# Two-layer hybrid decoder step: normalised x held two tiles ahead, channel-major projections, and score masks added on VectorE with the maximum

## The chip, the cores and the metric

The kernel runs on one core of one Trainium2 chip (trn2) as one program on all five engines: TensorE (PE), VectorE (DVE), ScalarE (ACT), GpSimd (POOL) and SyncE (SP, which only issues DMAs here). The metric is the device time of one execution in microseconds, the median of several executions. All arithmetic is float32, apart from a bfloat16 copy of the score masks and of the identity.

## What is computed

Two layers run over a prompt of 2,048 rows of 1,024 channels and over 8 single-row samples. The prompt is nearly all of the work. Per layer, cut to what matters:

```
def hybrid_layer(x, c, pos0, k_buf, v_buf, shift_prev, wkv0, conv_buf, h0, lp):
    mod = jax.nn.silu(c) @ lp["w_mod"] + lp["b_mod"]
    shift_m, scale_m, gate_m = jnp.split(mod, 3, axis=-1)
    h = rmsnorm(x, lp["norm_pre"]) * (1.0 + scale_m[:, None]) + shift_m[:, None]
    proj = h @ lp["w_in"]                                  # 1024 -> 2880
    qa, ka, va, ga, pb, gb, xc, gc = jnp.split(proj, IN_OFFSETS, axis=-1)
    ya = swa_banded(rope(qa), rope(ka), va, sinks) * jax.nn.silu(ga)     # group A
    yb = rwkv7_time_mix(pb, gb, shift_prev, wkv0, lp)                    # group B
    yc = rglru_mix(xc, gc, conv_buf, h0, pos0, lp)                       # group C
    y = jnp.concatenate([ya, yb, yc], axis=-1) @ lp["w_out"]             # 1024 -> 1024
    return x + gate_m[:, None] * rmsnorm(y, lp["norm_post"])

def sink_attention(s, mask, sinks, v, eq):       # A: 128 queries against 256 keys, 8 heads
    s = jnp.where(mask, s, -jnp.inf)
    m = jnp.maximum(jnp.max(s, axis=-1, keepdims=True), sink)
    p = jnp.exp(s - m)
    denom = jnp.sum(p, axis=-1, keepdims=True) + jnp.exp(sink - m)
    return jnp.einsum(eq, (p / denom).astype(v.dtype), v)

def wkv_step(s, inp):                            # B: one token, state 64 x 64 for each of 4 heads
    sa = jnp.einsum("bhvk,bhk->bhv", s, -kk)
    s = s * w[:, :, None, :] + sa[..., None] * (kk * a)[:, :, None, :] + v[..., None] * k[:, :, None, :]
    return s, jnp.einsum("bhvk,bhk->bhv", s, r)
# C: u = causal conv of width 4; gates = sigmoid(u @ block-diagonal w); h_t = a_t h_(t-1) + b_t
```

## The kernel before

The prompt is cut into 16 tiles of 128 rows per layer, 32 tiles in all. Both weight matrices of a layer lie in SBUF. Before the first tile of a layer the modulation vectors are computed; after its last tile the 8 samples are worked through. One loop iteration is one tile n, in which some steps of tile n+1 are already done (those under `if ahead`). Each engine has its own list of instructions, written out by hand in `program`; the lists meet at semaphores (`s[...]`), and an engine carries out its list strictly in the written order. So the order of the source is the order of the work.

A float32 product is two MATMUL records in the profile. A stationary operand (a weight load) is at most 128 x 128, and the moving operand at most 512 columns wide. `half` is the two halves of the partitions; products of 64 x 64 are issued for both halves in turn.

On PE one tile of before runs as follows:

- `vbT`, the low-rank products (L512) and the sum of squares of k (L517);
- projections by `fill` (L419: the tile's transposed input `hT` is stationary, the weights move, rows of tokens come out): Q (512 wide), XC with VA (384), GB with GC (512, with the product for the bonus, L528, in between); the two XC blocks are then transposed back to channels (L415);
- the small matrices of group B (L545 to L555) and five rounds that invert a triangular matrix: `squares(level)` (L566) and `multiply(level)` (L579), between which lie fill steps of GA, the gate products of group C (L602), the transposes of GB and GC and of q and k (L415). After each round ACT and DVE copy the squares out of PSUM (`power`, `power_T`) and DVE adds the product to Q (`product`, L1315);
- scores: `scores(j)` for j = 0, 1. For each of two banks a bfloat16 product of the identity with the mask (L627, 512 columns) sets the bank to 0 or -1e30, and two products of q and k (L630, 256 columns) accumulate on it. DVE takes the maximum (`maxima`, L1367) and ACT the exponentials straight from PSUM (`exps`, L1035);
- the recurrence over two chunks of 64 rows: `right_side` (L662, L664), DVE copies it with the sign changed (`rhs`, L1380), `solve` (L673), ACT copies, `next_state` and `outputs` (L685 to L703), DVE scales the state (`state`); between them the transposed probabilities (`probs`, L415) and `values` (L652);
- for tile n+1: x is normalised by DVE (`x_norm`, L1207) from the root that ACT took, transposed (`x_lo`, `x_hi`), and projected: R and K (512 wide), then V, WA and KA (448 wide), and 7 of those blocks transposed to channels after ACT has copied them out (`channels_rk`, `channels_vw`);
- the output projection `project` (L757), two halves of 512 columns, then the post-norm: ACT squares, DVE forms the mean, ACT the root, DVE the reciprocal (L1452 to L1456) and the output rows (L1457 to L1460), the last of which signals `o_ready`.

## Time and profile before

| what | value |
|---|---|
| runs | 3259.58, 3265.19, 3268.19 us |
| median | 3265.19 us |
| profiled execution | 3271.33 us |
| its span, first to last instruction | 3269.5 us |
| PE busy | 3017.4 us (92%) |
| DVE busy | 1750.7 us (54%) |
| ACT busy | 1429.8 us (44%) |
| POOL busy | 0.2 us, 4 instructions |

Busy time is the union of an engine's instructions. PE's matmuls are pipelined: a record lasts longer than the distance to the next one, so what a product costs is read from the start of a group to the start of the next, not from its duration. A wait that an engine spends while the end of its last record is still modelled as busy shows less than its full length for the same reason.

### The profile page before, as it was taken

The numbers are of one execution on the slowest core, as the hardware profiler recorded it, in microseconds if no ns is written. First come the engines' busy times: TensorE is split into PE (matmuls) and PEld (weight loads), VectorE is DVE, ScalarE is ACT, GpSimd is POOL, SyncE is SP. The second block draws the span as 40 slices with busy tenths as digits, with TensorE's granted clock in tenths as the row PEclk, the third lists the DMA queues.
The fourth block names the chain that finished last, engine by engine and source line by source line (L and its number), as shares of the span: only waits on it lengthen the run. The fifth ranks groups of instructions, "written<-read, shape, count | busy, mean of one in ns | idle before, by whom it ended". The sixth has DMA issues, their size and how long they took to land.

```text
span 3269.5 us, 62255 instructions
## 1 busy us (share of the span) xinstructions
PE 3017.4 (92%) x24404; PEld 1852.7 (57%) x24404; DVE 1750.7 (54%) x4385; ACT 1429.8 (44%) x3055; POOL 0.2 (0%) x4
## 2 busy tenths in 40 slices
PE   4899999999999999998649999999999999999986
PEld 3555556666655555665335555566666655555654
DVE  1455555556555555555414555555566555555554
ACT  0444445445544444544204444454455544445432
POOL 0000000000000000000000000000000000000000
PEclk7999999999999999999769999999999999999996
DMA  9000000000000000000370000000000000000001
GB/s 371 8 20 20 20 20 19 7 20 20 20 13 20 20 20 20 19 7 14 119 289 2 20 20 20 20 19 7 20 20 20 13 20 20 20 20 19 12 9 39
DMA packets 36847, 116.07 MB, mean 36 GB/s; under 512 B 13104, under 2 KB 16304, under 8 KB 36016
## 3 DMA queue, kind: packets, MB, share of 16 engines
q1 hardware_dynamic: 29136, 89.20, 7.8%
q10 hardware_dynamic: 7648, 26.04, 2.1%
q8 instruction: 38, 0.62, 0.1%
q14 instruction: 25, 0.20, 0.0%
HBM read 96.83 MB, written 18.41 MB: 35 GB/s over the span
## 4 chain that ended last, share of the span: by engine, by line
PE 75%; DVE 15%; issue 6%; DMA 2%; ACT 1%; ACTq 0%; DVEq 0%; SPq 0%
PE G L419 37%; PE M L757 14%; PE M L415 5%; PE G L652 4%; DVE small L1367 2%; DMA RB<-in_w_mod 2%; PE M L579 2%; PE M L566 2%; PE G L425 2%; DVE W L1291 1%; DVE RA L1332 1%; DVE Q L1315 1%; PE M L602 1%; PE M L512 1%; PE M L545 1%
## 5 line engine op out<-in xcount | busy, mean ns | idle before, releaser
L419 PE MATMUL G<-w_in,hT 128*128 128x512 f32 (+2 forms) x3072 | 1296.6, 572 | 3.1 <-DVE hT L1212 3.1
L419 PEld LDWEIGHTS G<-w_in,hT 128*128 128x128 f32 x3072 | 571.4, 191 | 552.8 <-issue 474.9
L757 PE MATMUL M<-w_out,yT 128*128 128x512 f32 x1024 | 454.1, 597 | 5.2 <-DVE yT L1446 5.2
L757 PEld LDWEIGHTS M<-w_out,yT 128*128 128x128 f32 x1024 | 191.3, 192 | 223.9 <-issue 223.9
L1224 DVE TENSOR_TENSOR xs<-pB 128x768 f32<-128x768 f32 x32 | 30.7, 959 | 395.8 <-ACT pB L938 395.8
L1315 DVE TENSOR_TENSOR Q<-Q,M 64x256 f32<-64x256 f32 x320 | 133.8, 418 | 119.4 <-PE M L579 115.3
L566 PE MATMUL M<-W 64*64 64x64 f32 x4608 | 163.5, 218 | 7.8 <-DVE W L1291 7.8
L566 PEld LDWEIGHTS M<-W 64*64 64x64 f32 x4608 | 149.4, 135 | 11.3 <-issue 11.3
L630 PE MATMUL M<-kT,stA 64*128 64x256 f32 x512 | 144.3, 402 | 0.0
L652 PE MATMUL G<-Vt,RB 128*128 128x64 f32 x1024 | 127.9, 278 | 0.0
L579 PEld LDWEIGHTS M<-Q,W 64*64 64x64 f32 x2560 | 88.2, 134 | 68.2 <-issue 68.2
L652 PEld LDWEIGHTS G<-Vt,RB 128*128 128x128 f32 x1024 | 119.1, 191 | 4.3
L1035 ACT ACTIVATE RA<-M,small 128x256 f32<-128x256 f32 x256 | 117.3, 472 | 0.0
L984 ACT ACTIVATE W<-M 64x512 f32<-64x512 f32 (+1 forms) x160 | 87.6, 547 | 66.6 <-PE M L566 66.6
L1070 ACT ACTIVATE RB<-M 128x512 f32<-128x512 f32 x32 | 19.1, 598 | 210.3 <-PE M L757 210.3
L972 ACT ACTIVATE xcb<-M 128x256 f32<-128x256 f32 x32 | 12.4, 386 | 222.8 <-PE M L415 222.8
L579 PE MATMUL M<-Q,W 64*64 64x64 f32 x2560 | 107.5, 223 | 2.5
L630 PEld LDWEIGHTS M<-kT,stA 64*128 64x128 f32 x512 | 85.6, 186 | 36.4 <-issue 29.0
L1309 DVE COPY W<-M 64x512 f32<-64x512 f32 (+1 forms) x160 | 102.0, 638 | 6.3
L1291 DVE TENSOR_TENSOR W<-M,nstrict 64x512 f32<-64x512 f32 x64 | 44.1, 689 | 111.1 <-PE M L545 110.6
L415 PE MATMUL M<-cst,RA 128*128 128x128 f32 x642 | 87.8, 284 | 6.4 <-DVE stA L1579 6.4
L927 ACT ACTIVATE stB<-G 128x320 f32<-128x320 f32 x32 | 14.0, 438 | 171.8 <-PE G L419 171.8
(403 smaller groups left out, 4559.2 us busy)
## 6 DMA issues: line engine op xcount, KB each, us to landing
w_in<-in_w_in SPq DMA_DIRECT2D x2, 11520.0 KB, 33.3
xa<-in_x_prompt SPq DMA_DIRECT2D x16, 512.0 KB, 3.6
RA<-in_w_mod ACTq DMA_DIRECT2D x16, 512.0 KB, 6.3
W<-in_w_mod ACTq DMA_DIRECT2D x16, 512.0 KB, 6.5
w_out<-in_w_out SPq DMA_DIRECT2D x2, 4096.0 KB, 36.7
G<-in_x_prompt SPq DMA_DIRECT2D x16, 512.0 KB, 3.3
x_mid<-RA SPq DMA_DIRECT2D x16, 512.0 KB, 2.8
xa<-x_mid SPq DMA_DIRECT2D x16, 512.0 KB, 3.7
```

The lines of the kernel that those rows point to most:

```text
L415: return nc.tensor.transpose(out, in_, ident[0:rows, 0:rows])
L419: last = mm(out[:, 0:width], hT[:, k, :], Win[:, k, col:col + width], start=k == 0, stop=k == KC - 1)
L566: last = mm(m[r, 256 * w + CH * u:256 * w + CH * u + CH], NW[r, 1 - w, u, :], NW[r, w, u, :], start=True, stop=True)
L579: last = mm(m[r, 256 + CH * u:256 + CH * u + CH], NW[r, 1, u, :], Q[r, u, :], start=True, stop=True)
L630: last = mm(m[:, 256 * c:256 * c + 256], qT[HD * g:HD * g + HD, 2 * j + c, :], kT[HD * g:HD * g + HD, :], start=False, stop=True, skip_gro ...
L652: last = mm(G1[:, HD * (4 * j + k):HD * (4 * j + k) + HD], PT[:, f, k, :], Vt[:, f, HD * g:HD * g + HD], start=f == 0, stop=f == 1)
L757: last = mm(o[:, :], yT[:, k, :], Wout[:, k, 512 * h:512 * h + 512], start=k == 0, stop=k == KC - 1)
L984: A(NW[half[0], w:], M0[half[0], 256 * w:512].rearrange("p (w u c) -> p w u c", u=U, c=CH), ACT.Copy).then_inc(s["inv_act"], 1)
L1035: last = A(Pm[:, j, k, :], m[:, 256 * (k // 2):256 * (k // 2) + 256], ACT.Exp, bias=small[:, 16 + 4 * j + k:17 + 4 * j + k], scale=SCALE, ...
L1291: last = tt(NW[r], m[r, :].rearrange("p (w u c) -> p w u c", w=2, c=CH), over(nstrict[r], 2, U), ALU.mult)
L1309: cp(NW[half[1], w:], M1[half[1], 256 * w:512].rearrange("p (w u c) -> p w u c", u=U, c=CH))\
L1315: last = tt(Q[r, :, :], Q[r, :, :], m[r, 256:512].rearrange("p (u c) -> p u c", c=CH), ALU.add)
```

## The change

Seven things are changed, in one go.

1. **x two tiles ahead.** `xn` is gone: DVE normalises x in place in `xa` (`x_mean`), for tile n+2, late in tile n. `hT` has two buffers, and the loop body is two tiles long. `x_lo` and `x_hi` of tile n+1 move from the recurrence to before `multiply(4)` and before `scores(0)`.
2. **Channel-major projections.** A new `channels` takes the weights as stationary operand and the 128 columns of `hT` as moving operand, so channels come out directly. R, K, V, XC, GB and GC (12 blocks of 128) are made so; Q and GA stay as `fill` of 512 columns, VA becomes a `fill` of 128, and WA with KA one of 192. Of the 13 transposes back to channels (4 for R and K, 3 for V and WA, 2 for XC, 4 for GB and GC) one is left (`wab`, for WA).
3. **Order on PE.** GB and GC are no longer projected early; their four blocks (`gates(0..3)`) stand inside the recurrence. The gate products of group C come after six of the eight steps of Q. The steps `vbT`, low rank and sum of squares of tile n+1 (`front`) stand between the halves of `project`.
4. **Masks on DVE.** The four mask products are gone. `maxima` is four `tensor_tensor_reduce`, each of which adds the mask to 256 columns, writes them to `Pm` in SBUF and gives their maximum. ACT takes the exponentials from `Pm`. In `scores` the two halves of the partitions alternate.
5. **Roots on POOL.** The roots of the pre-norm, of group B's norm and of the post-norm are a power of -0.5 on POOL, with their small sums before it. DVE's reciprocals after them are gone. Group B's squares move from ACT to DVE.
6. **Operands of B ahead.** The decays (ACT, 3 table loads) and `operands` (DVE) of tile n+1 stand at the end of tile n, ahead of the output rows.
7. **Smaller moves.** `rope` moves from before the inversion to after `power_T(2)`; the gates' silu on GA is split into a copy and a later silu; `power_T` now waits for the product of the round before.

The core of the diff, other moves left out:

```
+            def channels(out, H, col, width):
+                for k in range(KC):
+                    last = mm(out[0:width, :], Win[:, k, col:col + width], H[:, k, :], start=k == 0, stop=k == KC - 1)
+                return last
...
-                    fill(G0, C_Q, 512, range(KC)).then_inc(s["q_mm"], 1)
-
-                    fill(G1, C_XC, 384, range(KC)).then_inc(s["xv_mm"], 1)
-
-                    pe.wait_ge(s["q_out"], DONE(n))
-                    fill(G0, C_GB, 512, range(0, 5))
...
+                    for j in range(2):
+                        channels(G1[:, P * j:P * j + P], H, C_XC + P * j, P)
+                    fill(G1[:, 2 * P:3 * P], H, C_VA, P, range(KC)).then_inc(s["xv_mm"], 1)
+
+                    pe.wait_ge(s["rk_out"], DONE(n))
+                    fill(G0, H, C_Q, 512, range(0, 6))
+                    pe.wait_ge(s["conv_ready"], DONE(n))
+                    for k in range(4):
+                        last = mm(M3[:, P * k:P * k + P], gatew[:, k, :], lu[:, k % 2, :], start=True, stop=True)
...
-                        for g, m in ((0, ma), (1, mb)):
-                            mm(m[:, :].rearrange("p (c k) -> p c k", c=2), identb[:, :], over(mk[:, :], 1, 2),
-                               start=True, stop=False, skip_group_check=True)
-                            for c in range(2):
-                                last = mm(m[:, 256 * c:256 * c + 256], qT[HD * g:HD * g + HD, 2 * j + c, :],
-                                          kT[HD * g:HD * g + HD, :], start=False, stop=True, skip_group_check=True)
...
+                        for c in range(2):
+                            for g, m in ((0, ma), (1, mb)):
+                                last = mm(m[:, 256 * c:256 * c + 256], qT[HD * g:HD * g + HD, 2 * j + c, :],
+                                          kT[HD * g:HD * g + HD, :], start=True, stop=True)
...
-                        for g, m in ((0, ma), (1, mb)):
-                            last = red(mx[:, :, g], m[:, :].rearrange("p (c k) -> p c k", c=2), AX_X, ALU.max)
+                        dve.sem_inc(L["dve_w"], 1)
+                        for c in range(2):
+                            for g, m in ((0, ma), (1, mb)):
+                                last = nc.vector.tensor_tensor_reduce(
+                                    out=Pm[:, j, 2 * c + g, :], in0=m[:, 256 * c:256 * c + 256], in1=mk[:, :], scale=1.0,
+                                    scalar=NEG, op0=ALU.add, op1=ALU.max, accum_out=mx[:, c, g:g + 1])
...
+                    pool.wait_ge(s["o_squared"], DONE(n))
+                    link(tt(small[:, 5:6], small[:, 3:4], small[:, 4:5], ALU.add))
+                    pool.sem_inc(L["pool_w"], 1)
+                    link(ts(small[:, 5:6], small[:, 5:6], D * EPS, None, ALU.add))
+                    tt(small[:, 60:61], small[:, 5:6], minus, ALU.pow).then_inc(s["o_root"], 1)
...
-                    dve.wait_ge(s["o_squared"], DONE(n))
-                    link(tt(small[:, 5:6], small[:, 3:4], small[:, 4:5], ALU.add))
-                    link(ts(small[:, 5:6], small[:, 5:6], 1.0 / D, EPS, ALU.mult, ALU.add))
-                    assert link.k == OVAR, link.k
+                        operands(n + 1)
+
                     dve.wait_ge(s["o_root"], DONE(n))
```

**The recurrence on PE.** Before, from the second pair of scores to the first transposed probabilities (`mk,identb` is the mask product, `RH,Q` the solve, `cst,RA` the transposes of the probabilities):

```order
L627 MATMUL M<-mk,identb 128x512 [waits l_zeros]
L630 MATMUL M<-kT,stA 128x256 x2
L627 MATMUL M<-mk,identb 128x512
L630 MATMUL M<-kT,stA 128x256 x2
L662 MATMUL M<-S,kr 64x64 [waits s_qbd]
...
L664 MATMUL M<-Vst,G 64x64 x2
L668 REGISTER_ALU
L673 MATMUL M<-RH,Q 64x64 [waits s_rh_ready]
L673 MATMUL M<-RH,Q 64x64 x3
L415 MATMUL M<-cst,RA 128x128 [waits s_exp0]
```

and in the changed kernel (`hT,w_in` is `gates(0)`):

```order
L634 MATMUL M<-kT,stA 128x256 [waits s_inv_dve,s_inv_act,l_zeros]
L634 MATMUL M<-kT,stA 128x256 x3
L665 MATMUL M<-S,kr 64x64 [waits s_q_dve]
...
L667 MATMUL M<-Vst,G 64x64 x2
L438 MATMUL G<-hT,w_in 128x128 [waits s_hT_hi]
L438 MATMUL G<-hT,w_in 128x128 x7
L671 ISA
L676 MATMUL M<-RH,Q 64x64 [waits s_rh_ready]
L676 MATMUL M<-RH,Q 64x64 x3
L429 MATMUL M<-cst,RA 128x128 [waits s_exp0]
```

The masks have left, and eight products of 128 columns now stand between the right side and the solve that waits for DVE's copy of it.

**The gate products of group C on PE.** Before, in the second round of the inversion (`RA,gatew` are the gate products, `cst,stA` the transposes of GB and GC):

```order
L566 MATMUL M<-W 64x64 x16
L602 MATMUL M<-RA,gatew 128x128 [waits s_bt_out,s_conv_ready]
L602 MATMUL M<-RA,gatew 128x128 x3
L415 MATMUL M<-cst,stA 128x128 [waits s_gbc_out]
L415 MATMUL M<-cst,stA 128x128 x3
L419 MATMUL G<-w_in,hT 128x512 x2
```

and in the changed kernel, at the start of the tile:

```order
L438 MATMUL G<-hT,w_in 128x128 [waits s_pB_ready]
L438 MATMUL G<-hT,w_in 128x128 x15
L433 MATMUL G<-w_in,hT 128x128 x8
L433 MATMUL G<-w_in,hT 128x512 [waits s_rk_out]
L433 MATMUL G<-w_in,hT 128x512 x5
L544 MATMUL M<-RA,gatew 128x128 [waits s_conv_ready]
L544 MATMUL M<-RA,gatew 128x128 x3
```

The gate products, and the wait for the convolution with them, have moved ahead of the inversion, behind XC, VA and six steps of Q.

**The two maxima on DVE** of the changed kernel. Each `tensor_tensor_reduce` is compiled to two instructions, shown as ISA; the product of the fifth round (L1345) now stands ahead of them, and the transposed halves of hT (L1242) ahead of that:

```order
L1242 TENSOR_SCALAR hT<-G,gs,mod 128x128 [waits s_xT_hi]
L1242 TENSOR_SCALAR hT<-G,gs,mod 128x128 x3
L1345 TENSOR_TENSOR Q<-Q,M 64x256 [waits s_q_mm5]
L1345 TENSOR_TENSOR Q<-Q,M 64x256
L1394 ISA RA,small<-M,mk 128x256 [waits s_s0_mm]
L1394 ISA small 128x1
```

Before, the maxima of the first pair stood ahead of that product:

```order
L1367 TENSOR_REDUCE small<-M 128x2 [waits s_s0_mm]
L1367 TENSOR_REDUCE small<-M 128x2
...
L1371 TENSOR_SCALAR small<-small 128x4 [waits l_dve_t]
L1372 TENSOR_TENSOR small<-prm,small 128x4
L1315 TENSOR_TENSOR Q<-Q,M 64x256 [waits s_q_mm5]
L1315 TENSOR_TENSOR Q<-Q,M 64x256
```

## Rows read from the trace of the kernel before

**Rows 1.** The page's part 1, and TensorE's granted clock over 40 slices.
```profile
PE 3017.4 (92%) x24404; PEld 1852.7 (57%) x24404; DVE 1750.7 (54%) x4385; ACT 1429.8 (44%) x3055; POOL 0.2 (0%) x4
...
PEclk7999999999999999999769999999999999999996
```

**Rows 2.** Sums by stretch: both tile loops (from:to, length, busy times, clock, DMA).
```profile
150.00:1580.00 1430.00, 1378.82 (x11171) 844.29 (x11174) 806.06 (x1995) 666.87 (x1436) 0.00 (x0) 0.99 0.06 19
...
1760.00:3190.00 1430.00, 1379.85 (x11351) 847.32 (x11349) 813.60 (x2010) 678.51 (x1457) 0.00 (x0) 0.99 0.05 17
```

**Rows 3.** Waits of PE, all tiles: total us, times, longest.
```profile
PE M L602 <- DVE xcb L1335: 31.0, 32, 1.0
PE M L673 <- DVE RH L1380: 24.8, 32, 0.8
```

**Rows 4.** PE in order of time, gate products of two successive tiles (start, length, records).
```profile
774.38 1.16 PE L602 MATMUL M<-RA,gatew 128*128 128x128 f32 x8 [0.97 <-DVE xcb L1335]
775.38 0.60 PE L415 MATMUL M<-cst,stA 128*128 128x128 f32 x4
...
864.85 1.16 PE L602 MATMUL M<-RA,gatew 128*128 128x128 f32 x8 [0.97 <-DVE xcb L1335]
```

**Rows 5.** PE in order of time, scores to first probabilities, then `x_lo`.
```profile
789.69 0.39 PE L627 MATMUL M<-mk,identb 128*128 128x512 bf16 x1
790.01 1.13 PE L630 MATMUL M<-kT,stA 64*128 64x256 f32 x4
791.07 0.39 PE L627 MATMUL M<-mk,identb 128*128 128x512 bf16 x1
...
792.71 0.33 PE L662 MATMUL M<-S,kr 64*64 64x64 f32 x4 [0.20 <-DVE Q L1315]
...
793.08 0.31 PE L664 MATMUL M<-Vst,G 64*64 64x64 f32 x4
794.17 0.45 PE L673 MATMUL M<-RH,Q 64*64 64x64 f32 x8 [0.78 <-DVE RH L1380]
794.55 1.09 PE L415 MATMUL M<-cst,RA 128*128 128x128 f32 x8
...
796.90 0.28 PE L703 MATMUL M<-Vst,G 64*64 64x64 f32 x4
797.32 0.66 PE L415 MATMUL G<-cst,RA 128*128 128x128 f32 x4
```

**Rows 6.** PE in order of time, `values`, projection of R and K, transposes.
```profile
803.89 2.00 PE L652 MATMUL G<-Vt,RB 128*128 128x64 f32 x16
805.73 7.08 PE L419 MATMUL G<-w_in,hT 128*128 128x512 f32 x16
812.65 0.60 PE L415 MATMUL M<-cst,stA 128*128 128x128 f32 x4
813.09 0.60 PE L415 MATMUL M<-cst,W 128*64 128x128 f32 x4
```

**Rows 7.** DVE in order of time: post-norm, output rows; product, maxima of a pair.
```profile
744.62 0.16 DVE L1452 TENSOR_TENSOR small<-small 128x1 f32<-128x1 f32 x1 [2.44 <-ACT RB L1075]
...
746.40 0.75 DVE L1457 SCALAR_TENSOR_TENSOR RA<-M,small,gp 128x512 f32<-128x512 f32 x1
...
748.99 1.19 DVE L1245 COPY Vst<-M 64x128 f32<-64x128 f32 x4
...
791.72 0.84 DVE L1315 TENSOR_TENSOR Q<-Q,M 64x256 f32<-64x256 f32 x2
...
794.05 1.29 DVE L1367 TENSOR_REDUCE small<-M 128x2 f32<-128x512 f32 x2
```

**Rows 8.** ACT in order of time: one exponential and its accumulator read; a table load.
```profile
744.61 1.28 ACT L1077 ACT_TABLE_LOAD   x1
...
791.95 0.46 ACT L1035 ACTIVATE RA<-M,small 128x256 f32<-128x256 f32 x1
792.31 0.19 ACT L1035 ACTIVATION_READ_ACCUMULATOR RA<-M,small 128x1 f32 x1
```

647 lines of the change are left out of this document (338 added, 309 removed).

## Prediction

> **What bounds the kernel now.** I read the page's busy shares first [rows 1]: PE is busy for 92% of the span, DVE for 54%, ACT for 44%. The two tile loops alone, taken from the sums by stretch [rows 2], have PE at 1378.8 of 1430 us, 96%, at a granted clock of 0.99 (the 2.4 GHz level). Between two successive tiles the same instruction starts at 774.38 and at 864.85 [rows 4], so a tile takes 90.5 us, and 32 of them are 2,895 of the 3,269.5 us. PE is busy in about 87.2 us of a tile and idle in 3.3. So PE's list sets the time, and there are two ways to gain: less work on it, or fewer waits in it. A faster DVE or ACT gains nothing by itself. The clock cannot rise further.
>
> Then the waits of PE in a tile. The list of waits has two that occur 32 times [rows 3]: the gate products of group C wait for the convolution on DVE (31.0 us in all, 0.97 each), and the solve waits for DVE's sign change (24.8 us, 0.78). Both show a little short, since the modelled end of the record before covers part: from the start of L664 at 793.08, which takes about 0.12, to the solve at 794.17 there is 1.0 us [rows 5]. Two smaller ones are in the order of time: 0.2 before the right side, and about 0.3 before `x_lo` (from 796.90 to 797.32 less one group of 0.12) [rows 5]. With some tenths before the first squares and before the second right side, about 3.3 us.
>
> **PE's work, part by part.** Prices are distances from start to start, for one tile.
>
> Transposes: 13 go, 1 comes. Four take 813.09 - 812.65 = 0.44 us [rows 6], so 12 x 0.11 = **-1.3**.
>
> Masks: a mask product starts at 789.69, the score product after it at 790.01 [rows 5]. Four of 0.32: **-1.3**. The two kinds of products also alternate between two shapes of the array, and the first score record after a mask comes late, so up to -1.7.
>
> Narrow blocks: the 8 steps of 512 columns for R and K take 812.65 - 805.73 = 6.92 us [rows 6], or 1.73 for 128 columns. A block of 128 in `channels`, or VA's as `fill`, is 8 products of two records, each with a weight load of 128 x 128 of its own and 128 moving columns. No row has just that. The nearest from below is a transpose, 0.11 a record; from above the gate products, 8 records in 775.38 - 774.38 = 1.00, 0.125 each, with a late start in it [rows 4]. `values` has the same weight load, two records a product, and half the columns: 16 records in 1.84 us, 0.115 [rows 6]. It is nearest, because the load, and not the columns, seems to set its pace; I take 0.115. A block is then 1.84, and 13 of them (12 and VA) cost 13 x 0.11 = **+1.4**, between +0.4 (0.11) and +3.5 (0.125). WA and KA at 192 columns are taken at their share of the old 448.
>
> Shape changes: `gates(0)` stands between products of 64 x 64. Two changes of shape more, about 0.1 to 0.15 each: **+0.3**.
>
> Work together: -1.3 - 1.3 - 0.4 + 1.4 + 0.3, about **-1.3** (with the masks at -1.7).
>
> **PE's waits.** The wait for the convolution goes: in the new list XC, VA and six steps of Q stand before the gate products. From the end of `project`, PE has 3 x 1.84 + 6 x 0.865 = 10.7 us of its own. DVE needs the post-norm's root, the output rows (746.40 to 748.99, 2.6) [rows 7], the copies of V (1.2) [rows 7] and the convolution (about 2.8). With ACT's square of 0.8 before, 7.4 us are fixed, and a root chain of up to about 2.7 us on POOL is hidden after semaphores. **-1.0**.
>
> The wait of the solve goes: `gates(0)`, 1.84 us, stands in it. **-1.0**. The one before `x_lo` goes, since x is ready a tile earlier (**-0.3**), those before the two right sides too (**-0.4**): the fifth product now comes before the maxima on DVE, and `gates(1)` covers the state.
>
> One wait comes. The exponentials of the first pair are late, because `product(5)` now stands ahead of the maxima. From the end of `multiply(5)`: the product 0.85 [rows 7], four mask-and-maximum instructions, three small ones 0.35, the exponentials 4 x 0.45 + 0.2 = 2.0 [rows 8], hops 0.3. An add-and-maximum of 256 columns from PSUM is in no row. Two rows bound it: half a reduction of 512 columns (0.65 / 2 = 0.32) and the sum of half-width add (0.42, half of L1315's pair) and a whole reduction of its own (0.65), 1.07 [rows 7]. ACT's accumulator read, 0.19 and half hidden [rows 8], is what its second instruction is like, so I take 0.42 + 0.13 = 0.55. The chain is 0.85 + 2.2 + 0.35 + 2.0 + 0.3 = 5.7 us. PE has in that time scores (about 1.9 without masks), right side 0.5, `gates(0)` 1.84, solve 0.4, together 4.6. **+1.0 to +1.1**.
>
> Waits together: -1.0 - 1.0 - 0.3 - 0.4 + 1.05, about **-1.7**; following all four lists through one tile by these prices, with the late starts, gives PE **86.7 us** a tile where the same walk through the old lists gives 90.2 (trace: 90.5). That is -3.5, against -3.0 by the two sums above; the walk has the smaller waits that I rounded away. I take -3.5.
>
> What must stay hidden in it: `rope` (2.7 us on DVE) in the second round lies beside fill steps of GA and the third squares; table loads of ACT (1.28 each [rows 8]) fall from 12 to 8 a tile, the one in the third round ends before the third squares; decays, three loads and `operands` of tile n+1 lie beside the second half of `project`, 6.9 us, and end about 2 us after it, beside XC. On SP, x of tile n+2 is asked for after `x_hi` and is there long before ACT's square. If one of ACT's copies in the inversion were late by a load, PE would lose up to 1.3 a tile.
>
> A rule on the scores. Row first: the four records of a bank's scores come one after another, 790.01 to 791.07, 0.21 to 0.25 each plus a change of shape [rows 5]; all of them lie in one half of the rows of the array. In the change the halves alternate. The Trainium skill (TensorEngine Tiling (Array Packing), Key Properties) says that tiles of different row groups work independently, in parallel. By the rule a pair of scores would take about 1.1 us and not 1.9, and PE's busy time would fall by 1.7 a tile; but the same products and maxima on DVE then end the wait, so a tile would be 86.6 and not 86.7, and the time 3 us less.
>
> **The sum.** 32 x -3.5 = -112. The first tile of each layer now has decays and operands before its loop, some of it bare: +3 a layer, +6. Span 3269.5 - 112 + 6 = 3163.5. The profiled execution took 1.8 us more than its span and was 6.1 us above the median of the runs: 3163.5 + 1.8 - 6.1 = 3159. I round to **3158 us**, 3.3% less.
>
> **Rivals.**
>
> *The root chain on POOL is long.* Three POOL instructions with a power in the last. POOL has done only 4 fills of 0.05 us [rows 1], so no row bounds it above. From below it is about 0.5: the same sums on DVE take 0.16 each [rows 7]. Before, 1.8 us passed from the sum (744.62) to the output rows (746.40) [rows 7]. DVE waits for the root in order; behind it are output rows, the copies of V and the convolution, and PE's gate products wait for these. Up to 2.7 us nothing shows. At 4.5 us a tile costs 1.8 more: 3158 + 58 = 3216. The other roots have over 10 us of cover.
> The Trainium skill (GPSIMD Engine Reference, on how an instruction executes) gives POOL two software dispatch hops where VectorE has one, which speaks for this rival; it has no price for a power, and no run shows one yet.
>
> *Slower: the same mechanism further on.* Above 2.7 + 3.5 = 6.2 us for the three instructions the tile is longer than before. At 7.5 us each tile is 4.8 above forecast: 3158 + 154 = 3312. For it speaks that a power is no simple operation; against it that there is one value a partition.
>
> *The maxima are slow.* At 1.07 us for each of the eight instead of 0.55, the chains through them to the solve and to the exponentials grow by 2.1 and PE has nothing to put there: 3158 + 32 x 2.1 = 3225. It is at its worst 1.5 a piece, where the gain is gone.
>
> *The narrow blocks are not as cheap, or the waits merely move.* At 0.125 a record the blocks cost 2.1 more: 3225. A table load of ACT bare in the inversion in each tile: 3199. Both: 3266, no gain.
>
> **Chances.** Forecast 0.66 (own range 3105 to 3195); POOL long but hidden in part 0.11; POOL over 6.2 us 0.06; maxima slow 0.09; narrow blocks or a load bare 0.08. The low end has every unknown at its lower bound: narrow blocks at 0.11 (-1.0), maxima at 0.42 (-0.5), halves in parallel: 85.2 a tile, 3110; I set 3105. The high end takes in the rivals that are still faster: 3230. Outside lie 0.06 above for POOL, 0.04 for two rivals together and some below. A difference of 0.3% (10 us) is what a measurement can tell: faster 0.88, within 0.04, slower 0.08.
>
> **What would show it.** In the profile of the changed kernel: tiles 86 to 87 us apart; PE's wait before the gate products and before the solve gone; a wait of about 1 us before the first probabilities, ended by ACT's exponentials; 128-column records 0.11 to 0.125 apart; ACT with 8 loads a tile; the three POOL instructions within 2.7 us between ACT's second square and the output rows. Wrong if the gate products still wait for the convolution (POOL), if the solve waits for the sign change behind long maxima, or if a copy of ACT ends waits in the inversion.

## The result, and the profile after

The changed kernel takes 3142.7 us, the median of four runs (3135.95 to 3146.62). The kernel before took 3266.5 beside it (3259.58 to 3268.19). The ratio is 0.962, 95% interval 0.960 to 0.9645: 3.8% less, 15 us below the forecast of 3158 and inside its range. The profiled execution has a span of 3134.2 us, where that of before had 3269.5.

The page's part 1, then the sums over one tile (from:to, length, busy times, granted clock, DMA), of the changed kernel:

```profile
PE 2903.3 (93%) x29012; PEld 2200.6 (70%) x29012; DVE 1736.6 (55%) x4549; ACT 1216.0 (39%) x2739; POOL 108.2 (3%) x229
```
```profile
700.64:787.25 86.61, 84.43 (x862) 64.74 (x860) 51.48 (x133) 36.56 (x84) 3.38 (x7) 1.00 0.06 20
```

The same sum for the tile of before in [rows 4]:

```profile
774.38:864.85 90.47, 88.07 (x716) 53.91 (x717) 51.94 (x129) 43.36 (x93) 0.00 (x0) 1.00 0.05 18
```

Compare the last two. The tile is 3.86 us shorter (90.47 - 86.61). PE is busy 3.64 us less in it, and idle for 2.18 us instead of 2.40. So nearly all of the gain is work taken off PE's list, and hardly any of it is waiting. That is not how the forecast had it.

PE's waits, all tiles (total us, times, longest), of the changed kernel. The two of before [rows 3] were 31.0 for the convolution and 24.8 for the solve:

```profile
PE M L429 <- ACT RA L1022: 33.0, 32, 1.0
PE M L592 <- issue: 16.8, 32, 1.1
PE M L665 <- DVE Q L1345: 13.6, 30, 0.5
...
PE M L544 <- DVE xcb L1311: 6.7, 14, 0.6
```

Two waits of 32 times went; two of 32 and one of 30 came ("issue" at L592 is the semaphore of `power_T(5)`, below). The gate products still wait for the convolution, in 14 of 32 tiles.

PE in order of time from the first scores to the first probabilities, in the changed kernel; it answers to [rows 5]:

```profile
740.75 1.14 PE L634 MATMUL M<-kT,stA 64*128 64x256 f32 x8
742.37 0.68 PE L592 MATMUL M<-Q,W 64*64 64x64 f32 x16 [0.49 <-issue]
742.98 1.14 PE L634 MATMUL M<-kT,stA 64*128 64x256 f32 x8
744.57 0.33 PE L665 MATMUL M<-S,kr 64*64 64x64 f32 x4 [0.45 <-DVE Q L1345]
...
745.18 2.05 PE L438 MATMUL G<-hT,w_in 128*128 128x128 f32 x16
747.16 0.45 PE L676 MATMUL M<-RH,Q 64*64 64x64 f32 x8
748.65 1.09 PE L429 MATMUL M<-cst,RA 128*128 128x128 f32 x8 [1.03 <-ACT RA L1022]
```

The eight records of a pair of scores take about 1.1 us. In before a bank with its mask takes 791.07 - 789.69 = 1.38 [rows 5], a pair 2.76. The solve at 747.16 follows the block gates(0) without a wait.

DVE and ACT beside it:

```profile
739.88 0.85 DVE L1345 TENSOR_TENSOR Q<-Q,M 64x256 f32<-64x256 f32 x2 [0.99 <-PE M L592]
740.76 0.86 DVE L1382 TENSOR_TENSOR_SCAN lh<-RA,hcar 128x128 f32<-128x128 f32 x2
...
741.84 0.43 DVE L1339 COPY W<-M 64x256 f32<-64x256 f32 x1
742.30 1.37 DVE L1242 TENSOR_SCALAR hT<-G,gs,mod 128x128 f32<-128x128 f32 x4
743.59 0.84 DVE L1345 TENSOR_TENSOR Q<-Q,M 64x256 f32<-64x256 f32 x2
744.46 0.42 DVE L1394 CUSTOM_DVE_ANT_0 RA<-M,mk 128x256 f32<-128x256 f32 x1
...
744.81 0.42 DVE L1394 CUSTOM_DVE_ANT_0 RA<-M,mk 128x256 f32<-128x256 f32 x1
```
```profile
746.42 0.21 ACT L1020 ACTIVATE small<-small 128x4 f32<-128x4 f32 x1 [4.47 <-DVE small L1401]
```

DVE does not stop from 739.88 to the end of the maxima. All three new waits of PE hang on this list: the fifth multiply (L592) waits for L1339 (`power_T(5)`), the right side (L665) for L1345 (`product(5)`), and the probabilities (L429) for ACT, which begins when the maxima are through.

The distance from one tile to the next is 86.61 us and 87.3 to 87.4 us in turn, through both loops; below, a tile of the second kind is called slow. There are 12 of them among the 28 distances of the two layers. DVE at the start of a slow tile, the copies of V and the end of the convolution:

```profile
801.31 1.19 DVE L1298 COPY Vst<-M 64x128 f32<-64x128 f32 x4 [1.99 <-issue]
...
805.12 0.17 DVE L1311 COPY xcb<-xcb 128x6 f32<-128x6 f32 x1
```

At its loop's jump back DVE stands still for 1.99 us, waiting for no engine. The convolution then ends at 805.3 and PE's gate products start at 805.35, with a wait of 0.56. The kernel before has one tile in its loop's body, so it jumps back after every tile, and there DVE goes from the last output row straight to the copies of V, which start at 748.99 [rows 7]:

```profile
747.85 1.23 DVE L1460 TENSOR_TENSOR RA<-RA,G 128x1024 f32<-128x1024 f32 x1
```

So the stop came with the body of two tiles. What it consists of is not shown.

### The profile page after: what moved, and what is told of

Its sections match the earlier page's. It is cut to its first block, busy times and chain, and to the rows that moved or that the text cites. A ratio compares the mean times of both kernels' runs of the same rounds, so it can differ in the third digit from the quotient of the medians.

```text
span 3134.2 us, 71309 instructions
## 1 busy us (share of the span) xinstructions
PE 2903.3 (93%) x29012; PEld 2200.6 (70%) x29012; DVE 1736.6 (55%) x4549; ACT 1216.0 (39%) x2739; POOL 108.2 (3%) x229
## 4 chain that ended last, share of the span: by engine, by line
PE 66%; issue 18%; DVE 9%; DMA 3%; ACT 3%; POOL 1%; ACTq 0%; DVEq 0%; POOLq 0%; SPq 0%
PE G L438 15%; PE G L433 13%; PE M L765 8%; PE M L579 4%; PE G L655 4%; PE M L429 3%; PE M L592 2%; ACT RA L1022 2%; PE G L444 2%; PE M L433 2%; DVE Q L1345 1%; DVE hT L1242 1%; PE M L605 1%; PE M L560 1%; DVE RA L1394 1%
## 5 line engine op out<-in xcount | busy, mean ns | idle before, releaser
L438 PE MATMUL G<-hT,w_in 128*128 128x128 f32 x6144 | 739.0, 279 | 4.6 <-DMA w_in<-in_w_in 2.9
L438 PEld LDWEIGHTS G<-hT,w_in 128*128 128x128 f32 x6144 | 714.4, 193 | 26.5 <-issue 19.7
L433 PE MATMUL G<-w_in,hT 128*128 128x512 f32 (+1 forms) x1536 | 538.4, 494 | 0.0
L433 PEld LDWEIGHTS G<-w_in,hT 128*128 128x128 f32 x1536 | 236.6, 191 | 159.5 <-issue 152.9
L1345 DVE TENSOR_TENSOR Q<-Q,M 64x256 f32<-64x256 f32 x320 | 133.6, 417 | 117.6 <-PE M L592 114.5
L592 PEld LDWEIGHTS M<-Q,W 64*64 64x64 f32 x2560 | 88.2, 134 | 82.6 <-issue 82.6
L1022 ACT ACTIVATE RA<-RA,small 128x256 f32<-128x256 f32 x256 | 125.9, 495 | 0.0
L592 PE MATMUL M<-Q,W 64*64 64x64 f32 x2560 | 107.5, 223 | 16.8 <-issue 16.8
L1468 DVE COPY Ep<-M 64x256 f32<-64x256 f32 x64 | 26.7, 417 | 150.2 <-PE M L429 149.7
L429 PE MATMUL M<-cst,RA 128*128 128x128 f32 (+1 forms) x514 | 70.7, 280 | 39.4 <-ACT RA L1022 33.0
L1339 DVE COPY W<-M 64x512 f32<-64x512 f32 (+1 forms) x160 | 102.2, 639 | 5.7
L1271 DVE TENSOR_TENSOR_SCAN W<-cst,W 128x256 f32<-128x256 f32 x32 | 22.1, 692 | 147.8 <-ACT W L952 147.8
L926 ACT ACTIVATE pB<-G 128x512 f32<-128x512 f32 x32 | 19.1, 597 | 210.4 <-PE G L438 210.4
L1394 DVE CUSTOM_DVE_ANT_0 RA<-M,mk 128x256 f32<-128x256 f32 x256 | 93.3, 421 | 2.0
```

Of the source, the lines that this page charges most:

```text
L429: return nc.tensor.transpose(out, in_, ident[0:rows, 0:rows])
L433: last = mm(out[:, 0:width], H[:, k, :], Win[:, k, col:col + width], start=k == 0, stop=k == KC - 1)
L438: last = mm(out[0:width, :], Win[:, k, col:col + width], H[:, k, :], start=k == 0, stop=k == KC - 1)
L592: last = mm(m[r, 256 + CH * u:256 + CH * u + CH], NW[r, 1, u, :], Q[r, u, :], start=True, stop=True)
L1022: last = A(Pm[:, j, k, :], Pm[:, j, k, :], ACT.Exp, bias=small[:, 16 + 4 * j + k:17 + 4 * j + k], scale=SCALE, accum_out=small[:, 24 + 4 * ...
L1339: cp(NW[half[1], w:], M1[half[1], 256 * w:512].rearrange("p (w u c) -> p w u c", u=U, c=CH))\
```

## The experiments

Times are medians of four runs (ten for gates0_after_outputs, one for masks_between). The kernel before, run beside them, took 3264.1 us with halves_apart, masks_back and the two gates0 kernels, 3264.4 with wide_blocks, conv_first, pool_longer and scans_late, and 3259.9 with the others. "Tile" is the distance between the starts of `project` in two successive tiles (fast, slow of a pair) in the profile.

| kernel | median us | tile us |
|---|---|---|
| changed | 3142.7 | 86.61, 87.3 |
| halves_apart | 3147.4 | 86.61, 87.3 |
| masks_back | 3135.9 | 86.28, 87.0 |
| masks_between | 3173.8 (one run) | 87.70, 88.4 |
| gates0_after_solve | 3216.6 | 88.8, 89.4 |
| gates0_after_outputs | 3256.8 | 89.9, 91.3 |
| wide_blocks | 3132.4 | 86.12, 86.8 |
| conv_first | 3131.4 | 86.61, 86.61 |
| pool_longer | 3186.1 | 87.05, 90.7 |
| scans_late | 3108.5 | 85.57, 86.3 |
| masks_scans | 3115.3 | 85.68, 86.4 |
| combo_b | 3088.6 | 85.27, 85.27 |
| combo_c | 3081.2 | 84.97, 84.97 |

The tile is the sharper measure: the ratios of halves_apart, masks_back, wide_blocks and conv_first to the kernel before have 95% intervals that overlap the changed kernel's 0.960 to 0.9645, so the medians do not tell these from it. The start is what blurs the medians. The first `project` begins between 170 and 192 us in these profiles, and ahead of every tile PE waits 25 to 49 us for the DMA of `w_mod`, which the edits do not touch. In gates0_after_solve, gates0_after_outputs and pool_longer some tiles differ from the figures of the table (two of pool_longer take 89.0 where the others in their place take 90.7).

### Masks and scores

**halves_apart**

```diff
-                        for c in range(2):
-                            for g, m in ((0, ma), (1, mb)):
+                        for g, m in ((0, ma), (1, mb)):
+                            for c in range(2):
```

> The changed kernel with one thing undone: in a pair of scores the two products of one half of the rows stand together again, as before, instead of alternating. Theory A (the halves run in parallel, but DVE's chain product, maxima, exponentials sets when the first probabilities start): PE's busy time goes up by about 0.8 us a pair, 1.6 a tile, 50 us in all; the first pair's 0.8 goes mostly into the wait of 0.49 before the fifth multiply, the second's into the 0.45 before the right side and the 1.03 before the probabilities, so the time stays within 10 us of the changed kernel's 3143 us. Theory B (pairs take the same either way, the row groups do not overlap): PE busy unchanged too. Theory C (the pairs lie on the path): 0.8 to 1.6 us a tile, 3168 to 3194 us.

Tile 86.61, PE busy 2905.8 us against 2903.3. The pair's rows read the same, 1.14 us for eight records:

```profile
748.23 1.14 PE L634 MATMUL M<-kT,stA 64*128 64x256 f32 x8
```

Unchanged busy time was what theory B expected, but its reason, no overlap, does not hold. The trace has the eight records start in pairs, 13 ns apart, though the list has all of one half first. It does not name the half of a record, but before the change, where one half stood alone between two masks, its records started 0.22 to 0.32 us apart, so the two of a pair must be of different halves. They overlap in either order. The alternation that the change wrote does nothing.

**masks_back**

```diff
+                        for m in (ma, mb):
+                            mm(m[:, :].rearrange("p (c k) -> p c k", c=2), identb[:, :], over(mk[:, :], 1, 2), ...)
...
-                                last = nc.vector.tensor_tensor_reduce(...)
+                            last = red(mx[:, :, g], m[:, :].rearrange("p (c k) -> p c k", c=2), AX_X, ALU.max)
...
-                            last = A(Pm[:, j, k, :], Pm[:, j, k, :], ACT.Exp,
+                            last = A(Pm[:, j, k, :], m[:, 256 * (k // 2):256 * (k // 2) + 256], ACT.Exp,
```

> The changed kernel with part 4 undone but for the order of the halves: the mask is a bfloat16 product on TensorE again, DVE takes two maxima of 512 columns, ACT takes the exponentials from PSUM. Theory of the record's sum (a mask product is 0.32 us of PE's list, four a tile, with shape changes up to 1.7): 1.3 to 1.7 us a tile slower, 3185 to 3197 us. Rival (before the probabilities PE waits 0.49, 0.45 and 1.03 us for DVE and ACT anyway, and DVE's two reductions at 0.65 take what its four masked maxima at 0.345 do, 1.3 against 1.4): PE's busy time goes up by 1.3 or more a tile, about 45 us, and the time stays within 10 us of 3143.

PE's wait before the probabilities, all tiles of masks_back:

```profile
PE M L429 <- ACT RA L1026: 21.3, 32, 0.7
```

The theory of the sum fails and the rival holds on time: 3135.9 us, with the waits of 0.49 and 0.45 gone. PE's busy time rises by 28.6 us (2931.9), and not by the 45 of the rival. The tile is 0.33 us shorter, and so is the wait for the exponentials, 0.70 where the changed kernel has 1.03. The chain to them is shorter without the masks in it: from the first maximum to `rhs` DVE takes 1.67 us (757.73 to 759.40) where it took 1.85 (744.46 to 746.31), and ACT takes 1.91 for the exponentials, straight from PSUM, where it took 2.08 from SBUF.

**masks_between** is masks_back with the loops of before: mask, two products, mask, two products.

> The changed kernel with the scores exactly as before the change: the mask product of a bank directly ahead of its two score products, so that a mask product of all 128 rows of the array stands between the products of the two halves. With both mask products first, a pair's scores took 0.87 us for 8 records, two at a time; with the halves apart but no mask between them they took the same. Theory A (a product over all rows between the halves keeps them from overlapping): a pair takes 1.8 to 1.9 us again, PE's busy time is 25 to 30 us above that with both masks first (2932), the time within 10 us of it, since the fifth product on DVE is not ready earlier. Theory B (it makes no difference): busy 2932 within 5.

PE in order of time, masks_back and then masks_between, one pair of scores each:

```profile
756.25 0.61 PE L633 MATMUL M<-mk,identb 128*128 128x512 bf16 x2
756.79 1.13 PE L637 MATMUL M<-kT,stA 64*128 64x256 f32 x8
757.86 0.33 PE L668 MATMUL M<-S,kr 64*64 64x64 f32 x4
```
```profile
757.93 0.39 PE L633 MATMUL M<-mk,identb 128*128 128x512 bf16 x1
758.25 1.13 PE L636 MATMUL M<-kT,stA 64*128 64x256 f32 x4
759.31 0.39 PE L633 MATMUL M<-mk,identb 128*128 128x512 bf16 x1
759.63 1.13 PE L636 MATMUL M<-kT,stA 64*128 64x256 f32 x4
760.69 0.33 PE L667 MATMUL M<-S,kr 64*64 64x64 f32 x4
```

A pair is 1.61 us with both masks first and 2.76 with a mask between the halves. Without masks it is 1.1. So the two mask products cost 0.5 a pair, and the place of the second one another 1.15, since it keeps the halves from overlapping. That is 2.3 us a tile. Theory A on masks_between had the mechanism right and half of the size (PE busy 2999.7 us, 68 more than masks_back; its 0.87 for a pair's scores with the masks first is 1.07 in the rows above, 756.79 to 757.86). It was wrong on time, within 10 us: the tile is 87.70, 1.42 more than in masks_back, and the one run 38 us above that kernel's median. PE's list grew by 68 / 32 = 2.1 us a tile, and the only wait left to take that in was the 0.70 before the probabilities, which is gone in this run; here PE's own list is the path.

The masks as such are another matter. With both first on TensorE they are work for PE where it waited anyway. Moving them to DVE gained nothing by itself, it cost 0.33 us a tile (masks_back to the changed kernel); taking them from between the halves gained 1.42 (masks_between to masks_back).

### What the exponentials and the solve wait for

**gates0_after_solve**

```diff
-                    gates(0)
                     solve(0)
+                    gates(0)
```

> The changed kernel with the block gates(0) behind the first solve instead of before it. Theory of the record's sum (the wait of the solve, 1.0 us a tile, went away because gates(0) stands in it): the wait returns, 3143 + 32 = 3175 us. Rival (the exponentials' chain sets the start of the probabilities, and both places of gates(0) lie before it): PE waits about 1.1 us before the solve and nothing or 0.2 before the probabilities, the time stays within 10 us of 3143.

**gates0_after_outputs** puts gates(0) directly ahead of gates(1).

> The changed kernel with gates(0) behind the first outputs, next to gates(1), so that nothing of it stands before the first probabilities. Theory A (the probabilities start when the exponentials are done, whatever stands before): their start stays, PE idles there for the 1.8 us of the block besides, and the tile gets 1.8 us longer: 3143 + 58 = 3201 us. Theory B (PE's work alone counts, the block is only moved): 3143 within 10 us.

The time of both kernels lies above all theories on record (3216.6 us against 3175 and 3143, 3256.8 against 3201 and 3143). PE in gates0_after_solve, and the sums of short stretches around it (the number behind POOL's count is the granted clock):

```profile
514.12 0.69 PE L676 MATMUL M<-RH,Q 64*64 64x64 f32 x8 [1.78 <-DVE RH L1411]
514.75 3.19 PE L438 MATMUL G<-hT,w_in 128*128 128x128 f32 x16
517.77 1.04 PE L429 MATMUL M<-cst,RA 128*128 128x128 f32 x8
```
```profile
508.00:511.60 3.60, 2.71 (x32) 1.78 (x32) 3.48 (x11) 1.04 (x1) 0.00 (x0) 1.00 0.50 155
...
515.00:516.00 1.00, 1.00 (x6) 1.00 (x7) 0.87 (x7) 0.99 (x6) 0.00 (x0) 0.50 0.00 0
```

The wait is 1.78 and not 1.0, since on DVE the four maxima now stand between product(5), for which the right side waits, and `rhs`. After it TensorE's clock is at 0.50, the 1.2 GHz level, for about 3 us, and the block takes 3.02 from start to start where it took 1.98. That is so in most tiles: all 32 have the wait of 1.78, and in 29 the clock is down within the 3 us behind it. The rival was right that no wait is left before the probabilities: they are late by the slow block instead. Net of the 1.03 that is gone, the wait is 0.75 longer; the block adds 1.04 and the solve at the lower clock 0.25 (514.12 to 514.75, where it took 0.38 in [rows 5]), together 2.0 of the 2.2 us measured. In gates0_after_outputs a wait of 0.92 to 1.16 follows the 1.78, and the clock stays at 0.50 through the probabilities and the outputs: 3.3 us a tile in place of 1.8. Before the change, with waits of up to 1.0, the tile loops were at 0.99 [rows 2]. As a cover for the solve's wait gates(0) is worth 2.2 us a tile, twice what it was priced by; 0.75 of that is waiting and 1.3 is the clock.

**scans_late** moves the two scans and the copy of their last column on DVE:

```diff
                     product(4)
-                    for c in range(2):
-                        last = nc.vector.tensor_tensor_scan(lh[:, c, :], ...)
-                    link(last)
-                    cp(hcar[:, :].unsqueeze(2), lh[:, :, P - 1:P])
                     power_T(5)
...
                     rhs(0)
+                    for c in range(2):
+                        last = nc.vector.tensor_tensor_scan(lh[:, c, :], ...)
+                    link(last)
+                    cp(hcar[:, :].unsqueeze(2), lh[:, :, P - 1:P])
```

> The changed kernel with the two scans of group C and the copy of their last column (1.08 us on DVE) between the first rhs and the second maxima instead of ahead of power_T(5). Theory A (from the fourth product on, DVE's list is the path up to the first probabilities: power_T(5), h_hi, product(5), maxima, then ACT's exponentials): each of them starts 1.0 us earlier, PE's waits of 0.49 before the fifth multiply and of 0.45 before the right side go, and the tile is 1.0 us shorter, 3143 - 33 = 3110 us. Theory B (PE's own work sets the stretch, or the second maxima, now 1 us behind the first rhs, become late for the second exponentials): within 10 us of 3143.

```profile
741.70 0.68 PE L592 MATMUL M<-Q,W 64*64 64x64 f32 x16
...
743.42 0.33 PE L665 MATMUL M<-S,kr 64*64 64x64 f32 x4
...
747.50 1.09 PE L429 MATMUL M<-cst,RA 128*128 128x128 f32 x8 [1.03 <-ACT RA L1022]
```

Theory A, to 2 us: 3108.5, tile 85.57, both small waits gone, the one for the exponentials as it was. No instruction was removed. This shows that DVE's list is the path of this stretch, though DVE is busy for only 55% of the span.

**masks_scans** is masks_back and scans_late together.

> The changed kernel with the masks back on TensorE and the scans of group C behind the first rhs. With the masks back alone the tile was 0.33 us shorter than in the changed kernel, with the scans moved alone 1.04 shorter. Theory A (the mask products cost nothing there because PE waited before the fifth multiply; with the scans moved that wait is gone and the first pair's two mask products of 0.32 push the fifth multiply, product(5) and all behind it): 0.2 to 0.4 us a tile more than with the scans alone, about 85.9, 3118 us. Rival (the two effects add up): 85.2 a tile, 3098 us.

Tile 85.68. Adding the two effects would give 85.24, so they do not add, and the masks on TensorE now cost 0.11 instead of gaining 0.33. PE's list, now longer, starts the fifth multiply and the right side without a wait, and of the wait before the probabilities 0.22 is left (1.03 in scans_late). Theory A had the sign; the size is below its 0.2 to 0.4 by the tile, and at its low edge by the medians (6.8 us for 32 tiles).

### The narrow blocks, the convolution and POOL

**wide_blocks**

```diff
-                    for j in range(4):
-                        last = channels(G0[:, P * j:P * j + P], H, C_R + P * j, P)
-                    last.then_inc(s["rk_mm"], 1)
+                    fill(G0, H, C_R, 512, range(KC)).then_inc(s["rk_mm"], 1)
...
-                        return channels(G0[:, P * j:P * j + P], H, C_GB + P * j, P)
+                        return fill(G0, H, C_GB, 512, range(2 * j, 2 * j + 2))
```

> The changed kernel with R, K, GB and GC computed with the input as stationary operand and 512 moving columns (as before the change) but without the transposes, so that tokens and channels of these blocks are exchanged in what follows: it measures the pure price of the eight 128-column blocks. By the record's 0.115 us a record: 8 x 0.11 = 0.9 us of PE's list a tile, up to 28 us less, 3115. By 0.1125, as the changed kernel's rows read: 0.56 a tile, 14 to 18 us less, 3127. By the record's upper bound 0.125: 2.2 a tile, 3075 us. Half of the first gates block lies beside the exponentials' chain and gives nothing.

This kernel leaves out the transposes that the wide form needs, so what it computes is not the layer; only its time counts. Tile 86.12, 0.49 less, where 0.1125 us a record gives 0.56; the median is 10 us less, below the 14 to 18 of that line, and the prices of 0.115 and 0.125 are out. The changed kernel's own rows give the same: 64 records of R and K from 764.09 to 771.29, 7.20 us, where the wide form took 6.92 [rows 6]:

```profile
764.09 7.36 PE L438 MATMUL G<-hT,w_in 128*128 128x128 f32 x64
771.29 0.60 PE L429 MATMUL M<-cst,stA 128*128 128x128 f32 x4
```

**conv_first** moves DVE's four copies of V (L1298) behind the convolution, nothing else.

> The changed kernel with DVE's four copies of V (1.2 us) behind the convolution instead of ahead of it. In the changed kernel every second tile, the one whose start follows the loop's jump, is 87.3 to 87.4 us instead of 86.6: DVE stands still for 2.0 us at its jump, and the gate products wait 0.6 for the convolution. Theory A (that wait is all of the difference): the convolution ends 1.2 us earlier, all tiles are 86.6, 14 x 0.75 = 10 us less, 3133 us. Theory B (PE loses the 0.75 at a jump of its own, or in fetching instructions): the alternation stays and the time is unchanged.

Every tile is 86.61 us, and the median 11 us less. Theory A. DVE still stands still for 2.00 us at its jump, but the convolution now ends before PE needs it. So DVE's jump, by way of PE's wait for the convolution, is all of the alternation; PE jumps once in two tiles too and loses nothing.

**pool_longer**

```diff
+                    for _ in range(4):
+                        pool.sem_inc(L["pool_w"], 1)
+                        link(ts(small[:, 5:6], small[:, 5:6], 1.0, None, ALU.mult))
+                    pool.sem_inc(L["pool_w"], 1)
                     tt(small[:, 60:61], small[:, 5:6], minus, ALU.pow).then_inc(s["o_root"], 1)
```

> The changed kernel with four more multiplications by 1.0 in POOL's chain for the root of the post-norm, before the power: some 0.3 to 0.45 us each, so that the chain from ACT's second square to the root is 2.7 to 3.3 us instead of 1.6. The record's theory (up to 2.7 us the chain is hidden by PE's own work ahead of the gate products): 0 to 0.3 us a tile, 3143 to 3153 us. Rival (the cover is 1.4 us beyond what is used in one tile of two and nothing in the other, since DVE's jump of 2.0 us has used it up): 0 to 0.3 us in 16 tiles and 1.2 to 1.7 in 14, 3143 + 17 to 28 = 3160 to 3171 us.

POOL's chain in the changed kernel, then its first and last row in pool_longer, and there PE in a slow tile with the sums of the stretches behind the wait:

```profile
708.47 0.46 POOL L1144 TENSOR_TENSOR small<-small 128x1 f32<-128x1 f32 x1 [28.41 <-ACT RB L1063]
709.12 0.22 POOL L1146 TENSOR_SCALAR small<-small 128x1 f32<-128x1 f32 x1 [0.20 <-POOL small L1144]
709.43 0.57 POOL L1147 TENSOR_TENSOR small<-small,expo 128x1 f32<-128x1 f32 x1
```
```profile
724.20 0.46 POOL L1144 TENSOR_TENSOR small<-small 128x1 f32<-128x1 f32 x1 [28.41 <-ACT RB L1063]
...
726.86 0.57 POOL L1151 TENSOR_TENSOR small<-small,expo 128x1 f32<-128x1 f32 x1 [0.18 <-POOL small L1149]
```
```profile
645.36 1.86 PE L544 MATMUL M<-RA,gatew 128*128 128x128 f32 x8 [2.33 <-DVE xcb L1315]
```
```profile
645.30:647.00 1.70, 1.64 (x8) 1.64 (x9) 0.01 (x1) 0.00 (x0) 0.00 (x0) 0.60 0.00 0
647.00:649.70 2.70, 2.70 (x6) 1.22 (x5) 0.00 (x0) 1.14 (x4) 0.00 (x0) 0.62 0.00 0
```

The chain grew from 1.53 us (708.47 to 710.00) to 3.23. The fast tiles lost 0.45, so their cover ends at 1.53 + 1.7 - 0.45, about 2.8 us. The slow tiles lost 3.4. In the one shown the wait grew by 1.8, and after 2.33 us of idling the clock was at 0.60 and 0.62, so the gate products and two steps of Q took 1.65 and 2.74 where they take 1.0 and 1.73. In 2 of the 12 slow tiles the clock stayed at 1.00 behind a wait of 2.1, and those took 89.0 instead of 90.7. At 3186.1 us both theories are too low; the rival had the split right and missed the clock.

### A version that beats both

**combo_c** joins conv_first and scans_late with three more moves: `h_hi` goes from DVE to ACT, which waits 4.47 us there; the first maxima go ahead of product(5); gates(0) is cut in two.

```diff
-                    pe.wait_ge(s["q_dve"], STEP(n, 5, 5))
-                    right_side(0)
                     if ahead:
                         pe.wait_ge(s["hT_hi"], DONE(n + 1))
-                    gates(0)
+                    channels(G0[:, 0:P], H, C_GB, P, range(0, 4))
+                    pe.wait_ge(s["q_dve"], STEP(n, 5, 5))
+                    right_side(0)
+                    channels(G0[:, 0:P], H, C_GB, P, range(4, KC))
                     solve(0)
```

> A version meant to beat both: the changed kernel with (1) the convolution ahead of the copies of V, (2) the scans of group C behind the first rhs, (3) the upper half of hT (h_hi) on ACT, which is idle there, instead of DVE, (4) on DVE the first maxima ahead of product(5), (5) gates(0) cut in two, four products before the first right side and four behind it. Theory A (between the fourth product and the first probabilities the tile is bound by DVE's list, and after (2) by product, maxima, exponentials in a row): the exponentials are done about 1.2 us earlier than with (2) alone, each half of gates(0) covers one of the two waits (product(5), rhs), PE waits for nothing there, and a tile is 84.3 us: 3143 - 10 - 33 - 40 = 3060 us. Rival (ACT's table load, behind h_hi now, or the second maxima come late): the gain of (3) to (5) is lost, 3097 us.

**combo_b** leaves gates(0) whole, ahead of the right side.

> As the version with gates(0) cut in two, but gates(0) stands whole before the first right side, and the solve right behind that. Theory A: all of it the same, but the solve waits some 0.7 us bare for DVE's rhs, 0.6 to 0.7 us a tile more than with the cut block: about 3082 us, and since the wait is under those after which the granted clock fell (1.78 and 2.33 us), it stays at the 2.4 GHz level. Rival (a wait of this length in this place lowers the clock too): more than 1 us a tile above the version with the cut block, over 3092 us.

```profile
745.00 1.13 PE L634 MATMUL M<-kT,stA 64*128 64x256 f32 x8
746.06 1.16 PE L438 MATMUL G<-hT,w_in 128*128 128x128 f32 x8
747.50 0.33 PE L665 MATMUL M<-S,kr 64*64 64x64 f32 x4 [0.28 <-DVE Q L1349]
...
748.11 1.16 PE L438 MATMUL G<-hT,w_in 128*128 128x128 f32 x8
...
749.58 1.09 PE L429 MATMUL M<-cst,RA 128*128 128x128 f32 x8
```

combo_c takes 3081.2 us, ratio 0.945 (0.943 to 0.946) to before, 2% less than the changed kernel, between theory A's 3060 and the rival's 3097. The wait before the probabilities is gone and 0.28 is left before the right side. The tile is 84.97 and not the 84.3 of theory A. That price took 1.25 us out of a stretch where only 1.03 of waiting was left in scans_late; 0.6 came out. Of the other 0.43, 0.28 is the wait that is left and 0.15 is time of PE's own list, by my reading the changes of shape around the cut block, which no run tests by themselves. combo_b is 0.30 a tile longer, less than theory A's 0.7, and its wait of 0.79 left the clock at 1.00 in all 32 tiles. Single shares of the three moves were not measured.

## Why the prediction was right, and where it was not

**The size of a tile.** 3.5 us less was forecast; 3.86 came in tiles of 86.61, about 3.1 in those after DVE's jump, 3.7 in the mean of the 28 distances within the layers. The last tile of each layer gained 7.4 (84.24 to 76.84), which the sum had not priced apart. The total adds up in the profiles: 60.0 and 58.6 us between the first and the last `project` of the two layers, 1.2 at the layer boundary, 0.5 at the end, and 15.1 ahead of the first `project`. Of the last, 11.4 us lie ahead of the first product with `w_in` (85.12 us before, 73.72 after), where PE waits for the DMA of `w_mod`. They cannot be put down to the change, since that point varies from 73.7 to 95.5 us between kernels that are the same up to it. The other 3.7 are the first tile. Without the 15.1 it is 120.3 us where the sum had 112 - 6 = 106. The difference is some 6 in the loops, 8 in the last tiles, and the 6 that the starts of the layers were to cost and did not (the boundary is 1.2 shorter), less the two distances that 32 tiles do not have. That is about the size by which the result fell below the forecast.

**The work on PE.** Forecast -1.3, measured -3.64. The transposes stand. The masks with the shape changes at -1.7 are the term that was mis-sized: a pair went from 2.76 to 1.1, 3.3 a tile. The missing 1.6 is the overlap of the halves. The rule of the Trainium skill (TensorEngine Tiling (Array Packing), Key Properties) that tiles of different row groups work in parallel was weighed for exactly this and left out of the sum; the trace agrees with it. But it was tied to the alternation, and halves_apart shows that this is not what brings the overlap: masks_between shows that the full-height mask product between the halves had prevented it. The prediction also held that the overlap would be worth 3 us in all, since DVE's chain then ends the wait. No run has the changed kernel's form, without masks on TensorE and without the overlap, so that is not tested. With the masks on TensorE the overlap is worth 1.4 a tile (masks_between against masks_back, 3173.8 against 3135.9 us); the new waits of 0.49 and 0.45 suggest that without the masks it is worth less.

**Narrow blocks.** +1.4 was taken at 0.115 us a record. At 0.1125 it is 12 x 0.06 to 0.07 and VA, some +0.9. The mechanism was right, and so was the row taken as the nearest.

**The waits.** Forecast -1.7, measured -0.2. The sum started from 3.3 us of idling in a tile, out of windows that hold more than the tiles; the tile of before has 2.40, so there was less to take away. Three of the steps hold: the convolution's wait went (in fast tiles), the solve's went, the exponentials' came, at 1.03 against 1.0 to 1.1. What failed is the step "those before the two right sides too (-0.4), the fifth product now comes before the maxima": DVE's list ahead of the fifth product holds the scans, `power_T(5)` and `h_hi`, and PE, which the overlap made faster, waits 0.49 and 0.45 for it. And gains entered one by one do not add where they share a path: masks_back gains 0.33, scans_late 1.04, and both together (masks_scans) 0.93. From the fourth product to the probabilities the changed kernel has one path, and it runs through DVE.

**Maxima.** Bounded by 0.32 and 1.07, taken as 0.55, measured 0.345 from one to the next (744.46, 744.81). The wait for the exponentials came out right all the same, and that is luck. The chain was forecast at 5.7 us from the end of the fifth multiply and took 5.67 (742.98 to 748.65): the four maxima took 0.8 less, and product(5) began 0.6 late, held up by DVE's list. PE's part was forecast at 4.6 and took 4.56: the scores took 0.8 less, and the wait before the right side, the right side and gates(0) took the rest back.

**POOL.** 1.53 us, inside the 2.7 that was to be hidden, and 2.8 is where fast tiles begin to pay. In slow tiles the cover was already gone by 0.56, since DVE's jump was not in the sum. The rivals with a long chain did not come true; pool_longer shows that they had the right mechanism and a price too low, since after the wait of 2.33 us most of PE's next 4 us of work went at half the clock.

**ACT.** It loads 8 tables a tile, as forecast, and none of them shows in PE's waits inside the inversion.

So the time was right for reasons that were partly others. The overlap (1.6 us a tile) was missing from the sum, and so were the two new waits (0.9) and the jump (0.75 in 12 tiles); the waits that went were taken as larger than they were. These nearly cancelled. That the total came within 15 us is in part luck.

## What to carry to other kernels

Read which engine's list is the path in each stretch before pricing an edit there: where an engine waits anyway, more work on it costs nothing and less work gains nothing, and reordering another engine's list, with no instruction less, can gain time (34 us here for moving three instructions). Products on different halves of the rows overlap when nothing of full height stands between them, so group the full-height ones. When a cover for a wait is moved, price the clock too, not only the wait.

## What the runs showed of the hardware

- TensorE's clock: after PE had idled for 1.78 us within a busy loop, the granted clock was 0.50 (1.2 GHz) for about 3 us; after 2.33 us, 0.60 in the mean of the 1.7 us behind it. It does not fall every time: in 3 of 32 tiles it stayed up behind 1.78 us, in 2 of 12 behind 2.1. After all 32 waits of 1.03 in the changed kernel, and of 0.79 in combo_b, it stayed at 1.00. In the tiles shown the clock cost about 1.3 us on top of the wait in gates0_after_solve and about 1.65 in pool_longer.
- Products on the two halves of the rows, issued four and four, start in pairs 13 ns apart (halves_apart): a half does not wait for the records of the other half ahead of it in the list. One full-height product between them ends that: 2.76 us for a pair of scores with its masks, against 1.61 with both masks first.
- DVE stands still for 1.9 to 2.0 us at each of the 12 jumps of its two-tile loop. In the kernel before, whose loop holds one tile, it does not stop at the jump, and PE, at its own jump, shows no gap. The Trainium skill (Advanced Engine Details and Errata, Control Flow Timing) gives a compare-and-branch about 108 ns; the trace shows far more on DVE, and no run here tells what the rest is. A loop's jump belongs where its engine has time.
- A power on POOL costs 0.57 us for one value a partition and 1.04 for four; the add before it 0.44.
- An add with maximum over 256 columns from PSUM on DVE costs 0.345 us from one to the next, and its accumulator read is inside that.
